# Modulation units behind one counter, placed over more stages, and their quadrants added in five parts, in a two-block transformer kernel in fp32 on one core

## The chip, the cores and the metric

One core of one Trainium2 chip. The metric is the device time of one launch in microseconds (us), the median of repeated runs. A matrix product runs on TensorE (PE); VectorE (DVE), ScalarE (ACT) and GpSimd (POOL) work beside it, and SyncE (SP) issues most of the transfers.

## The reference, cut to what matters

Two models follow one another, each two layers deep, on 256 tokens of width 1024, all in fp32. The first has multi-head latent attention, sliding-window attention, and squared-ReLU MLPs. The second has a gated convolution and recurrence layer, then a stick-breaking attention layer, both with SwiGLU feed-forwards. Each layer of the second is modulated by a vector that depends on `c` alone:

```python
def ada_modulation(c, ada_w, ada_b):                 # c: (1, 1024), ada_w: (1024, 6144)
    m = jax.nn.silu(c) @ ada_w + ada_b
    return jnp.split(m, N_MOD, axis=-1)              # six vectors of 1024

def even_layer(x, c, ada_w, ada_b, mix_norm, w_in, ...):
    sh_m, sc_m, g_m, sh_f, sc_f, g_f = ada_modulation(c, ada_w, ada_b)
    h = modulate(rms_norm(x, mix_norm), sh_m, sc_m)
    ...
    x = x + g_m[:, None, :] * y
    hf = modulate(rms_norm(x, ffn_norm), sh_f, sc_f)
    return x + g_f[:, None, :] * swiglu(hf, ffn_w_gate, ffn_w_up, ffn_w_down)
```

The odd layer does the same with its own `ada_w`. Each of the two `ada_w` matrices is 24 MB; they are multiplied by one vector.

## The kernel before, in words

**The weights' ring.** Activations lie transposed: features on the partitions, 256 tokens in a row. Every large weight streams through a ring of two slots. For a slot SP loads `raw`; ScalarE rounds it to `w_hi` in two halves (`split`, L745, which waits for the load and for TensorE's earlier use of the slot); VectorE subtracts, `w_lo = raw - w_hi` (`split`, L1260, also two halves); TensorE multiplies three times for each chunk, hi by hi, hi by lo and lo by hi (L2172, L2173, L2174). A full slot is a block of 96 matmuls of 128x256, half of them for one pair of feature rows, half for the other (`two_bank_slot`, L2234). It waits for both halves of `w_lo`, and for the earlier contents of its PSUM banks to have been taken (`wait_acc`).

**The order of work.** All engines run programs written out by hand, in the same order of stages: w_o0, up0, down0, swa, w_o1, up1, down1 of the first model (`mlp` holds up and down, `swa` is the sliding-window layer); then lru_in, gate_up0, ffn_down0, qkv, the stick-breaking attention, sb_out, gate_up1, ffn_down1 of the second. Within an engine nothing overtakes: an instruction that waits holds up all behind it. `add_to_residual` and `add_gated` (L1464) on VectorE add the products to `xT`; the norm's first pieces follow from that (L1441 is the last step of the residual sum, L2053 the sum in ffn_down).

**Modulation.** The product with `ada_w` is not done on TensorE but on VectorE, in 96 units. A unit is one transfer of 512 KB (issued by POOL, `ada_load`, L571, into one of two buffers; it waits until unit m - 2 has been used) and two operations on VectorE (`ada_unit`, L1758 or L1761) that multiply by a column of silu(c) and add. Four units make one of 24 groups. A finished group (`ada_group_done`) is transposed into PSUM bank 7 (L1779) and reduced (L1782) into `ada_part`; the semaphore `ada_summed` counts groups. PSUM bank 7 is shared with the scores of the sliding-window heads, so TensorE waits for `ada_summed` ahead of `heads(16, 32)`. Of a finished layer `ada_combine` (four small matmuls, L2230) adds the quadrants into the norm bank, and `modulation` on VectorE adds the bias (L1789) and makes the gains of the two norms (L1791).

A table, `ADA_GROUP`, gives each stage its fixed units, in pairs (`ada_units`): a pair in each of w_o0's two turns, in each j of up and down, and so on. In up, gate_up0 and the turns of ffn_down VectorE's program is a hardware loop (`Fori`) around `hidden` or `turns`. `ada_combine(0)` runs inside up1, behind its fourth slot; `ada_combine(1)` in ffn_down0 behind the first `down`; `modulation(0)` stands in down1 at j = 1, `modulation(1)` in ffn_down0.

Where the pairs stand on VectorE's queue: in w_o0 and w_o1 the second pair stands behind all sums and ahead of `mlp`, whose first act is `split(Slot("up", 1))`. In down0 and down1 the pair of j = 7 stands ahead of the sum of the second turn's first two banks. In swa one pair stands behind split 2, ahead of the distances and the second queries; the other stands behind split 3, ahead of `swa_kT` (L1884), the keys of heads 16 and on. ScalarE swaps their halves (L1037) before TensorE forms the scores of heads 16 and 17 (L2422, `score_head`), for which it waits for `k_ready`.

## Time and profile before

| what | value |
| --- | --- |
| median of 3 runs | 1190.78 us (1190.17, 1190.78, 1193.43) |
| the profiled execution's own time | 1182.13 us |
| its span in the trace | 1180.5 us |
| TensorE busy | 1156.9 us, 98% of the span |
| VectorE busy | 881.7 us, 75% |
| ScalarE busy | 634.3 us, 54% |
| GpSimd busy | 95.6 us, 8% |
| moved by the DMA engines | 248.97 MB, mean 211 GB/s |
| granted TensorE clock | full in all of the 40 slices |

Busy time is the union of the records of an engine's instructions; matmuls are pipelined, so their records overlap, and 98% is not 98% of the peak. A row of a timeline gives the start, the length, the engine and line, the tiles and shapes, and in square brackets how long the engine was idle before and what ended that. The trace has one profiled execution, whose time is not the median's.

### The profile page before, as it was taken

How to read it: one execution, taken by the hardware profiler on the slowest of the kernel's cores; microseconds unless marked ns; L12 is line 12 of the kernel's file. 1: busy time of each engine (PE TensorE's matmuls, PEld its weight loads, DVE VectorE, ACT ScalarE, POOL GpSimd, SP SyncE). 2: the span in 40 equal slices, each digit the busy share in tenths (PEclk: the TensorE clock that was granted, in tenths of full speed). 3: DMA queues.
4: the chain of work that ended last, by engine and by line, in shares of the span. 5: the costliest groups of instructions: out<-in, count | busy, mean ns of one | idle time of the engine just before them, and what ended most of it. 6: DMA issues, size and time to landing. Idle time of an engine off the chain costs nothing.

```text
span 1180.5 us, 23101 instructions
## 1 busy us (share of the span) xinstructions
PE 1156.9 (98%) x9525; PEld 1119.7 (95%) x9525; DVE 881.7 (75%) x1174; ACT 634.3 (54%) x853; POOL 95.6 (8%) x147
## 2 busy tenths in 40 slices
PE   8999999999989999999999999999999999999998
PEld 8999999999988999999999999999988879999998
DVE  5876898878876798888998888887576557855543
ACT  7558566633347567634468463443455574634332
POOL 0000011111124011111200001010000000000000
PEclk9999999999999999999999999999999999999999
DMA  9352588887772488788844657877645504565462
GB/s 329 138 179 73 190 292 272 312 308 235 263 267 72 157 275 305 273 302 294 306 167 143 198 159 253 281 265 240 207 165 172 199 1 143 186 206 180 146 196 85
DMA packets 150060, 248.97 MB, mean 211 GB/s; under 512 B 5553, under 2 KB 80922, under 8 KB 149978
## 3 DMA queue, kind: packets, MB, share of 16 engines
q1 hardware_dynamic: 135858, 197.17, 49.6%
q0 software_dynamic: 13952, 50.60, 11.8%
q8 instruction: 60, 0.98, 0.4%
q14 instruction: 22, 0.18, 0.0%
q10 hardware_dynamic: 168, 0.04, 0.0%
HBM read 246.74 MB, written 1.05 MB: 210 GB/s over the span
## 4 chain that ended last, share of the span: by engine, by line
PE 67%; DVE 17%; ACT 4%; issue 3%; DMA 3%; POOL 0%; DVEq 0%; POOLq 0%; ACTq 0%
PE ps L2172 19%; PE ps L2173 19%; PE ps L2174 19%; DVE w_lo L1260 7%; DVE scratch L1761 4%; DMA ada_raw<-in_l_ada_w 3%; ACT w_hi L745 2%; PE ps L2454 2%; PE ps L2320 1%; PE ps L2764 1%; PE ps L2436 1%; DVE ps L1779 1%; ACT h_both L812 1%; PE ps L2738 1%; PE ps L2423 1%
## 5 line engine op out<-in xcount | busy, mean ns | idle before, releaser
L1260 DVE TENSOR_TENSOR w_lo<-raw,w_hi 128x2048 fp32r<-128x2048 f32 (+4 forms) x196 | 412.7, 2144 | 88.4 <-ACT w_hi L745 87.9
L745 ACT ACTIVATE w_hi<-raw 128x2048 fp32r<-128x2048 f32 (+4 forms) x196 | 342.2, 1791 | 156.4 <-PE ps L2174 151.9
L2172 PE MATMUL ps<-h_both,w_hi 128*128 128x256 f32 (+1 forms) x1296 | 360.6, 278 | 7.9 <-DVE w_lo L1260 4.4
L2173 PE MATMUL ps<-h_both,w_hi 128*128 128x256 f32 (+1 forms) x1296 | 358.8, 277 | 0.0
L2174 PE MATMUL ps<-h_both,w_lo 128*128 128x256 f32 (+1 forms) x1296 | 358.7, 277 | 0.0
L2172 PEld LDWEIGHTS ps<-h_both,w_hi 128*128 128x128 f32 (+1 forms) x1296 | 242.7, 187 | 9.9 <-issue 5.0
L2173 PEld LDWEIGHTS ps<-h_both,w_hi 128*128 128x128 f32 (+1 forms) x1296 | 243.4, 188 | 0.1
L2174 PEld LDWEIGHTS ps<-h_both,w_lo 128*128 128x128 f32 (+1 forms) x1296 | 242.7, 187 | 0.0
L2172 PE MATMUL ps<-a_both,w_hi 128*128 128x256 f32 x864 | 238.8, 276 | 0.6 <-DVE xT L2053 0.6
L2173 PE MATMUL ps<-a_both,w_hi 128*128 128x256 f32 x864 | 238.5, 276 | 0.0
L2174 PE MATMUL ps<-a_both,w_lo 128*128 128x256 f32 x864 | 238.5, 276 | 0.0
L2172 PEld LDWEIGHTS ps<-a_both,w_hi 128*128 128x128 f32 x864 | 162.2, 188 | 0.8 <-DVE xT L2053 0.8
L2173 PEld LDWEIGHTS ps<-a_both,w_hi 128*128 128x128 f32 x864 | 162.2, 188 | 0.0
L2174 PEld LDWEIGHTS ps<-a_both,w_lo 128*128 128x128 f32 x864 | 162.2, 188 | 0.0
L1761 DVE SCALAR_TENSOR_TENSOR scratch<-ada_raw,silu_c,scratch 128x512 f32<-128x512 f32 x168 | 126.2, 751 | 13.6 <-DMA ada_raw<-in_l_ada_w 6.1
L571 POOL DMA_DIRECT2D ada_raw<-in_l_ada_w x96 | 69.5, 724 | 623.6 <-DVE scratch L1761 623.3
L1153 ACT ACTIVATE a_both<-a_full 128x512 fp32r<-128x512 f32 x18 | 11.4, 633 | 107.5 <-DVE a_full L2038 107.5
L1007 ACT ACTIVATE a_full<-ps 128x512 f32<-128x512 f32 x32 | 19.0, 595 | 51.2 <-PE ps L2174 51.1
L2172 PE MATMUL ps<-h_wide,w_hi 128*128 128x258 f32 x160 | 45.8, 286 | 0.2 <-DVE xT L1441 0.2
L2173 PE MATMUL ps<-h_wide,w_hi 128*128 128x258 f32 x160 | 45.4, 284 | 0.0
L2174 PE MATMUL ps<-h_wide,w_lo 128*128 128x258 f32 x160 | 45.3, 283 | 0.0
L2172 PE MATMUL ps<-w_hi,h_both 128*128 128x512 f32 (+1 forms) x112 | 42.8, 382 | 0.7 <-issue 0.7
(423 smaller groups left out, 1806.6 us busy)
## 6 DMA issues: line engine op xcount, KB each, us to landing
ada_raw<-in_l_ada_w POOLq DMA_DIRECT2D x96, 512.0 KB, 6.9
raw<-in_mlp_w_up SPq DMA_DIRECT2D x32, 1024.0 KB, 6.4
raw<-in_mlp_w_down SPq DMA_DIRECT2D x32, 1024.0 KB, 6.9
raw<-in_l_ffn_w_gate SPq DMA_DIRECT2D x22, 1024.0 KB, 5.4
raw<-in_l_ffn_w_up SPq DMA_DIRECT2D x22, 1024.0 KB, 8.6
raw<-in_l_ffn_w_down SPq DMA_DIRECT2D x16, 768.0 KB, 6.0
raw<-in_l_w_qkv SPq DMA_DIRECT2D x12, 1024.0 KB, 6.9
raw<-in_l_w_in SPq DMA_DIRECT2D x10, 1024.0 KB, 6.3
```

The lines of the kernel that those rows point to most:

```text
L571: pool.dma_start(ada_raw[:, slot, :, :], ada[l][:, 2 * quarter:2 * quarter + 2, group])\
L745: nc.scalar.activation(w_hi[:, s.slot, cut], raw[:, s.slot, cut], ACT.Copy).then_inc(split_hi, 1)
L812: ins = nc.scalar.activation(h_hi[:, ch, :], xT[:, ch, :], ACT.Copy, scale=col_a[:, gain_at + ch:gain_at + ch + 1])
L1007: nc.scalar.activation(full, acc(b if j else FIRST_UP_BANKS[b]).rearrange("p (c t) -> p c t", c=2), ACT.Relu)\
L1260: nc.vector.tensor_tensor(w_lo[:, s.slot, cut], raw[:, s.slot, cut], w_hi[:, s.slot, cut].bitcast(F32), ALU.subtract).then_inc(split_lo, 1)
L1761: ins = nc.vector.scalar_tensor_tensor(ada_sum, w, c, ada_sum, ALU.mult, ALU.add)
L1779: nc.vector.transpose(ps[:, ADA_BANK, :], ada_sum).then_inc(ada_turned, 1)
L2172: nc.tensor.matmul(to, sh, mh, start=first, stop=False, skip_group_check=True)
L2173: nc.tensor.matmul(to, sh, ml, start=False, stop=False, skip_group_check=True)
L2174: return nc.tensor.matmul(to, sl, mh, start=False, stop=last, skip_group_check=True)
L2320: ins = nc.tensor.transpose(ps[0:ncols, bank, ch * T + t * P:ch * T + (t + 1) * P], src(ch, t), ident[:, :])
L2454: ins = nc.tensor.matmul(ps[:, 6 + g % 2, qt * T + j * HD:qt * T + (j + 1) * HD], p[:, n * P:(n + 1) * P], v, start=j == 0 and n == 0, sto ...
```

## The change

One counter, `ada_begun`, hands out the units in order: `ada_units(n)` runs the next n, and closes a group with every fourth. The stages take other numbers of units than before (the calls in the diff), and `UP_UNITS` gives those of the up stages. VectorE's hardware loops are written out. `MOD_PARTS` cuts the 24 groups into five parts (first group, end, which gain is made): each has its own `ada_combine(k)` on TensorE and `modulation(k)` on VectorE, and `mod_kept` keeps a combine from writing over a part that VectorE has not taken. POOL's loads keep their order; they are cut at other points around its other work.

```diff
-ADA_GROUP = {"w_o0": 0, "up0": 1, "down0": 5, "swa": 9, "w_o1": 10, "up1": 11, "down1": 15, "gate_up0": 19}
+MOD_PARTS = ((0, 8, 0), (8, 12, 1), (12, 18, 0), (18, 22, 1), (22, 24, None))
+UP_UNITS = ((1, 1, 2, 2, 2, 2, 2, 2), (1, 1, 1, 2, 2, 2, 1, 2))
...
-            ada_loads(0, 10)
+            ada_loads(0, 8)
...
-            ada_loads(10, 11)
+            ada_loads(8, 11)
             ada_pair(11, 1)
             ada_pair(12, 0)
-            ada_loads(12, 19)
+            ada_loads(12, 15)
...
-            ada_loads(19, 23)
-            ada_pair(23, 1)
+            ada_loads(15, 21)
...
             nc.gpsimd.tensor_copy(denied[:, :], suffix[:, :]).then_inc(pool_step, 1)
+            ada_loads(21, 23)
+            ada_pair(23, 1)
...
-            def ada_units(phase, j, i=None):
-                slot_no = 2 * ADA_GROUP[phase] + j
...
-                for u in range(2):
-                    ada_unit(grow(4, 2 * slot_no + u), u, 2 * (j % 2) + u, grow(32, 16 * (slot_no + 1)))
-                if j % 2:
-                    layer = ADA_GROUP[phase] > ADA_GROUP["w_o1"] if i is not None else slot_no // 2 >= ADA_GROUPS
-                    ada_group_done(grow(1, slot_no // 2 + 1), ADA_SLOTS if layer else 0)
...
+            ada_begun = [0]
+            def ada_units(n):
+                for m in range(ada_begun[0], ada_begun[0] + n):
+                    ada_unit(m)
+                    if m % 4 == 3:
+                        ada_group_done(m // 4)
+                ada_begun[0] += n
+            def ada_group_done(g):
+                dve.wait_ge(ada_step, 8 * (g + 1))
                 nc.vector.transpose(ps[:, ADA_BANK, :], ada_sum).then_inc(ada_turned, 1)
...
+                dve.wait_ge(ada_turned, g + 1)
+                nc.vector.tensor_reduce(ada_part[:, g % ADA_GROUPS, :], ps[:, ADA_BANK, :].rearrange("p (b k) -> p b k", k=32),
+                                        AX.X, ALU.add).then_inc(ada_summed, 1)
...
-            def modulation(l):
...
-                dve.wait_ge(ada_combined, l + 1)
-                link(nc.vector.tensor_tensor(mod[:, l, :], ps[:, NORM_BANK, T:T + 48], col_b[:, c:c + 48], ALU.add))
...
+            def modulation(k):
+                first, last, which = MOD_PARTS[k]
+                l, at, n = first // ADA_GROUPS, 4 * (first % ADA_GROUPS), 4 * (last - first)
+                c = COL_B[f"ada_b{l}"] + at
+                dve.wait_ge(ada_combined, k + 1)
+                nc.vector.tensor_tensor(mod[:, l, at:at + n], ps[:, NORM_BANK, T:T + n], col_b[:, c:c + n], ALU.add).then_inc(mod_kept, 1)
+                dve.wait_ge(mod_kept, k + 1)
+                if which is not None:
+                    key = ("mix", "ffn")[which] + str(l)
+                    link(nc.vector.scalar_tensor_tensor(modg[:, l, which, :], mod[:, l, 8 + 24 * which:16 + 24 * which], 1.0,
+                                                        col_a[:, COL_A[key]:COL_A[key] + KD], ALU.add, ALU.mult))
...
             split(Slot("w_o0", 1))
-            ada_units("w_o0", 0)
+            ada_units(2)
             add_to_residual("w_o0", 0, following="mlp0")
             split(Slot("w_o0", 2))
             add_to_residual("w_o0", 1, following="mlp0")
-            ada_units("w_o0", 1)
             def mlp(l):
...
                 split(Slot(f"up{l}", 1))
                 delayed_sum(f"mlp{l}", 3)
...
-                def hidden(i):
...
-                                ada_units(f"up{l}", j, i)
-                        split(Slot(f"up{l}", j + 2, i, 2))
-                hidden(None)
+                def hidden(j):
...
+                        if b == 0:
+                            ada_units(UP_UNITS[l][j])
+                    split(Slot(f"up{l}", j + 2))
+                for j in range(2):
+                    hidden(j)
...
-                hidden(1)
-                if l:
-                    dve.wait_ge(ada_combined, 1)
-                with dve.Fori(2, 4) as i:
-                    hidden(i)
-                for j in range(8):
+                for j in range(2, 8):
+                    hidden(j)
+                for j in range(7):
                     if l and j == 1:
...
-                    ada_units(f"down{l}", j)
+                    ada_units(2)
                     following = ("attn1", "final")[l]
                     if j == 3:
                         add_to_residual(f"down{l}", 0, following, pairs=(0,))
-                    if j < 7:
-                        split(Slot(f"down{l}", j + 2))
+                    split(Slot(f"down{l}", j + 2))
                     if j == 3:
                         add_to_residual(f"down{l}", 0, following, pairs=(1,))
...
             swa_queries(0)
             split(Slot("swa", 2))
-            ada_units("swa", 0)
+            ada_units(2)
...
             swa_queries(1)
             split(Slot("swa", 3))
-            ada_units("swa", 1)
             wait_part(Slot("swa", 2), 0)
             nc.vector.tensor_tensor(swa_kT[:, :, :], two(SWA_BANKS[2][0]), row_pair, ALU.mult).then_inc(acc_out[0], 1)
...
             split(Slot("swa", 5))
-            ada_units("w_o1", 0)
+            ada_units(2)
             add_to_residual("w_o1", 0, following="mlp1")
             split(Slot("swa", 6))
             add_to_residual("w_o1", 1, following="mlp1")
-            ada_units("w_o1", 1)
             mlp(1)
...
             split(Slot("lru_in", 3))
+            modulation(1)
             for b in range(2):
...
-                    if l == 0:
-                        ada_units(f"gate_up{l}", j - 2, i)
+                    if j < 10 or l == 0:
+                        ada_units(2 - l)
                     dve.wait_ge(parts_done, s.before + 2)
...
-                with dve.Fori(1, 4) as i:
-                    for j in range(2):
-                        hidden(j, i)
-                for j in (8, 9, 10):
+                for j in range(2, 11):
                     hidden(j)
...
-                if l == 0:
-                    ada_units("gate_up0", 9)
-                    split(Slot("ffn_down0", 2))
-                    add(0)
-                    split(Slot("ffn_down0", 3))
-                    modulation(1)
-                    turns(1)
-                else:
-                    turns(0)
+                if l:
+                    modulation(4)
+                for i in range(3):
+                    if l == 0:
+                        ada_units(2)
+                    split(Slot(f"ffn_down{l}", 2 * i + 2))
+                    add(i)
+                    split(Slot(f"ffn_down{l}", 2 * i + 3))
+                    if l == 0 and i == 0:
+                        modulation(2)
                 if l == 0:
...
                 if j < 5:
                     split(Slot("qkv", j + 2))
+                if 1 <= j < 5:
+                    ada_units(1)
             def capped(pair):
...
             split(Slot("sb_out", 1))
+            modulation(3)
             add_gated("sb_out", 0, 1, "ffn1")
...
-            def ada_combine(l):
-                pe.wait_ge(quadrants_ready, 1)
-                pe.wait_ge(ada_summed, ADA_GROUPS * (l + 1))
-                first = 1 - l
...
+            def ada_combine(k):
+                first, last, _ = MOD_PARTS[k]
+                pe.wait_ge(ada_summed, last)
+                if k:
+                    pe.wait_ge(mod_kept, k)
+                at, n = first % ADA_GROUPS, 4 * (last - first)
+                part = ada_part[:, at:at + last - first, :].rearrange("p g (c j) -> p (g c) j", j=4)
...
+                with pe.Fori(1, 4) as i:
+                    two_bank_slot(f"up{l}", 0, i, 2)
+                    two_bank_slot(f"up{l}", 1, i, 2)
                 if l:
-                    for j in (2, 3):
-                        two_bank_slot("up1", j)
+                    pe.wait_ge(quadrants_ready, 1)
                     pe.wait_ge(norm_var, NORM_AT["mlp1"] + 1)
                     ada_combine(0)
-                with pe.Fori(1 + l, 4) as i:
-                    two_bank_slot(f"up{l}", 0, i, 2)
-                    two_bank_slot(f"up{l}", 1, i, 2)
...
-            pe.wait_ge(ada_summed, 10)
+            pe.wait_ge(ada_summed, 8)
...
             lru_slot(1, second_free)
+            pe.wait_ge(norm_var, NORM_AT["final"] + 1)
+            ada_combine(1)
             lru_slot(2, taken((0, 1), (1, 0)))
...
+                if l:
+                    ada_combine(4)
                 if l == 0:
                     down(0)
-                    ada_combine(1)
+                    ada_combine(2)
                     with pe.Fori(1, 4) as i:
                         down(i)
                 else:
...
                 pe.wait_ge(w_exped, 2 * pair + 2)
+                if pair == 2:
+                    pe.wait_ge(ada_summed, 22)
...
             as_chunks_arrive("sb_out", 3)
+            ada_combine(3)
             two_bank_slot("sb_out", 1)
```

## Rows read from the trace of the kernel before

**Rows 1.** The page, part 1: busy us, share of the span, instructions of each engine.

```profile
PE 1156.9 (98%) x9525; PEld 1119.7 (95%) x9525; DVE 881.7 (75%) x1174; ACT 634.3 (54%) x853; POOL 95.6 (8%) x147
```

**Rows 2.** Timeline, VectorE in `gate_up1`: start, us, operation, idle before and its releaser.

```profile
1039.29 0.69 DVE L2038 TENSOR_TENSOR a_full<-a_full,ps 128x512 f32 x1 [3.19 <-PE ps L2174]
...
1050.18 0.69 DVE L2038 TENSOR_TENSOR a_full<-a_full,ps 128x512 f32 x1 [3.20 <-PE ps L2174]
```

**Rows 3.** Timeline, TensorE: first matmuls behind five pauses.

```profile
151.61 0.39 PE L2172 MATMUL ps<-h_both,w_hi 128*128 128x256 f32 x1 [1.96 <-DVE w_lo L1260]
...
317.23 0.36 PE L2172 MATMUL ps<-h_both,w_hi 128*128 128x256 f32 x1 [1.66 <-DVE xT L1441]
...
350.25 0.34 PE L2422 MATMUL ps<-swa_kT,swa_qT 64*128 64x128 f32 x1 [3.34 <-DVE qx L1890]
...
421.49 0.38 PE L2172 MATMUL ps<-h_both,w_hi 128*128 128x256 f32 x1 [1.94 <-DVE w_lo L1260]
...
587.56 0.39 PE L2172 MATMUL ps<-h_wide,w_hi 128*128 128x258 f32 x1 [0.18 <-DVE xT L1441]
```

**Rows 4.** Timeline, ScalarE: split ahead of `up0` 1, and swapped keys in `swa`.

```profile
142.02 3.71 ACT L745 ACTIVATE w_hi<-raw 128x2048 fp32r<-128x2048 f32 x2
...
349.52 0.63 ACT L1037 ACTIVATE swa_kT_swapped<-swa_kT 64x512 f32<-64x512 f32 x1
```

**Rows 5.** Timeline, VectorE behind the sums of w_o0.

```profile
142.50 3.18 DVE L1761 SCALAR_TENSOR_TENSOR scratch<-ada_raw,silu_c,scratch 128x512 f32<-128x512 f32 x4
...
147.08 4.48 DVE L1260 TENSOR_TENSOR w_lo<-raw,w_hi 128x2048 fp32r<-128x2048 f32 x2
```

**Rows 6.** Timeline, VectorE at the end of down0, and in `swa`.

```profile
311.09 3.18 DVE L1761 SCALAR_TENSOR_TENSOR scratch<-ada_raw,silu_c,scratch 128x512 f32<-128x512 f32 x4 [1.36 <-DMA ada_raw<-in_l_ada_w]
...
343.49 3.22 DVE L1761 SCALAR_TENSOR_TENSOR scratch<-ada_raw,silu_c,scratch 128x512 f32<-128x512 f32 x4 [2.42 <-DMA ada_raw<-in_l_ada_w]
...
348.11 0.68 DVE L1884 TENSOR_TENSOR swa_kT<-ps,r_row 128x512 f32<-128x512 f32 x1
```

**Rows 7.** Timeline, VectorE in `gate_up0`: splits of two slots in turn.

```profile
774.28 4.49 DVE L1260 TENSOR_TENSOR w_lo<-raw,w_hi 128x2048 fp32r<-128x2048 f32 x2 [1.00 <-ACT w_hi L745]
...
784.70 4.49 DVE L1260 TENSOR_TENSOR w_lo<-raw,w_hi 128x2048 fp32r<-128x2048 f32 x2 [1.11 <-ACT w_hi L745]
```

**Rows 8.** Timeline, TensorE: around a combine; stick-breaking's first sums; `sb_out` block 0's end.

```profile
454.60 0.28 PE L2174 MATMUL ps<-h_both,w_lo 128*128 128x256 f32 x1
...
455.09 0.39 PE L2172 MATMUL ps<-h_both,w_hi 128*128 128x256 f32 x1
...
940.76 0.48 PE L2764 MATMUL ps<-sb_sp,suffix 128*128 128x384 f32 x1
...
980.77 0.28 PE L2174 MATMUL ps<-h_both,w_lo 128*128 128x256 f32 x1
```

**Rows 9.** Timeline, VectorE: `modulation` in ffn_down0, the stick-breaking's begin, `sb_out`.

```profile
820.46 0.20 DVE L1789 TENSOR_TENSOR mod<-ps,col_b 128x48 f32<-128x48 f32 x1
820.69 0.24 DVE L1791 SCALAR_TENSOR_TENSOR modg<-mod,col_a 128x8 f32<-128x8 f32 x2
...
934.05 1.02 DVE L2138 TENSOR_SCALAR sb_l<-ps 128x384 f32<-128x384 f32 x2 [0.63 <-PE ps L2742]
...
936.28 1.01 DVE L2147 TENSOR_TENSOR sb_sp<-ps,sb_l 128x384 f32<-128x384 f32 x2
...
979.73 0.87 DVE L1464 SCALAR_TENSOR_TENSOR xT<-ps,mod,xT 128x256 f32<-128x256 f32 x2 [2.76 <-PE ps L2174]
```

**Rows 10.** Windows: stretch, length, busy of PE, PEld, DVE, ACT, POOL, clock, DMA share, GB/s.

```profile
346.00:351.00 5.00, 1.66 (x17) 1.27 (x15) 3.48 (x6) 2.08 (x3) 3.57 (x7) 1.00 1.03 390
816.00:862.00 46.00, 45.45 (x406) 45.22 (x402) 25.05 (x26) 20.33 (x17) 0.00 (x0) 1.00 0.64 217
```

**Rows 11.** Timeline, ScalarE in ffn_down0.

```profile
810.59 2.66 ACT L745 ACTIVATE w_hi<-raw 128x1408 fp32r<-128x1408 f32 x2 [4.46 <-DMA raw<-in_l_ffn_w_down]
...
832.06 2.65 ACT L745 ACTIVATE w_hi<-raw 128x1408 fp32r<-128x1408 f32 x2 [4.83 <-PE ps L2174]
```

More of the change, by code:

```diff
@@ L1750, in _, with ada_unit @@
             ada_sum = scratch[:, 2:4, :].rearrange("p c t -> p (c t)")
[L1752 to L1754 removed]
+            def ada_unit(m):
+                slot, quarter = m % 2, m % 4
+                dve.wait_ge(ada_loaded[slot], 16 * (m // 2 + 1))
                 for q in range(2):
@@ L1810, in mlp @@
                 delayed_sum(f"mlp{l}", 3)
-                def hidden(i):
-                    grow = (lambda per, first: first) if i is None else (lambda per, first: i * per + first)
-                    for j in range(2):
-                        for b in range(2):
-                            at_pair = bass.ds(i * 8 + (4 * j + 2 * b), 2) if i is not None else slice(4 * j + 2 * b, 4 * j + 2 * b + 2)
-                            dve.wait_ge(hid_hi, grow(4, HIDDEN_BEFORE[str(l)] + 2 * j + b + 1))
-                            nc.vector.tensor_tensor(a_lo[:, at_pair, :], a_full[:, at_pair, :],
-                                                    a_hi[:, at_pair, :].bitcast(F32), ALU.subtract).then_inc(hid_lo, 1)
-                            if b == 0:
-                                ada_units(f"up{l}", j, i)
-                        split(Slot(f"up{l}", j + 2, i, 2))
-                hidden(None)
+                def hidden(j):
+                    for b in range(2):
+                        at_pair = slice(4 * j + 2 * b, 4 * j + 2 * b + 2)
+                        dve.wait_ge(hid_hi, HIDDEN_BEFORE[str(l)] + 2 * j + b + 1)
+                        nc.vector.tensor_tensor(a_lo[:, at_pair, :], a_full[:, at_pair, :],
+                                                a_hi[:, at_pair, :].bitcast(F32), ALU.subtract).then_inc(hid_lo, 1)
+                        if b == 0:
[3 more added lines that the diff above has]
+                    hidden(j)
                 delayed_var(f"mlp{l}")
@@ L2061, in ffn @@
                 split(Slot(f"gate_up{l}", 3))
-                with dve.Fori(1, 4) as i:
-                    for j in range(2):
-                        hidden(j, i)
-                for j in (8, 9, 10):
+                for j in range(2, 11):
                     hidden(j)
-                def turns(first):
-                    with dve.Fori(first, 3) as i:
-                        split(Slot(f"ffn_down{l}", 2, i, 2))
-                        add(i)
-                        split(Slot(f"ffn_down{l}", 3, i, 2))
-                if l == 0:
-                    ada_units("gate_up0", 9)
-                    split(Slot("ffn_down0", 2))
-                    add(0)
-                    split(Slot("ffn_down0", 3))
-                    modulation(1)
-                    turns(1)
-                else:
-                    turns(0)
+                if l:
[8 more added lines that the diff above has]
+                        modulation(2)
                 if l == 0:
```

46 lines of the change are left out of this document (12 added, 34 removed).

## The prediction

> **What bounds the kernel now.** I read the page's first part first. TensorE is busy 98% of the span, VectorE 75% [rows 1]. Matmuls overlap in the records, so the busy share doesn't say how dense TensorE is; the starts of its matmuls do. In `gate_up1` VectorE waits for each block of 96 matmuls, from 1039.29 to 1050.18 [rows 2]: 10.89 us, 0.113 us for each. Elsewhere the starts keep that step but for a few marked pauses. So TensorE sets the time, and a change is worth what it takes from, or adds to, the pauses between its matmuls; VectorE's load matters only where a pause names it.
>
> Next I read TensorE's timeline at the borders of stages. A pause costs its idle time plus 0.17 us (the record before it runs 0.28 us, of which 0.11 is its step). Five pauses stand in front of work that VectorE delivers late [rows 3]:
> - 151.61, block 1 of `up0`, waits for a split: 1.96 + 0.17 = 2.1 us. 421.49 is the same place of the next layer: 2.1 us.
> - 317.23, first matmul of `swa`, waits for the residual sum: 1.8 us. 587.56 is its twin before `lru_in`: 0.35 us.
> - 350.25, the scores of heads 16 and 17: 3.5 us. The row names the queries (L1890); but the swapped keys, which the scores need too, end at 349.52 + 0.63 = 350.15 [rows 4], 0.1 us before.
>
> Together 9.9 us.
>
> Then I read what VectorE did in front of each. At 142.50 it runs two units (four operations, 3.18 us) and closes a group, and only at 147.08 begins the split [rows 5], though ScalarE began its half of that split at 142.02 [rows 4]. At 311.09 two units come after 1.36 us of waiting for their transfer, and the residual sum stands behind them; at 343.49 another pair has waited 2.42 us for its transfer, and `swa_kT` (348.11) stands behind it [rows 6]. At all five places modulation units, whose result is needed much later, run ahead of something that TensorE awaits.
>
> **The change, part by part.** The units stay 96, the groups 24. A pair costs VectorE 3.2 us, closing a group 147.08 - 142.50 - 3.18 = 1.4 us more [rows 5]. Units per stage, before and after: w_o0 4, 2; up0 16, 14; down0 16, 14; swa 4, 2; w_o1 4, 2; up1 16, 12; down1 16, 14; gate_up0 18, 18; ffn_down0 2, 6; qkv 0, 4; gate_up1 0, 8.
>
> *w_o0 and w_o1:* the second pair goes, so the split of `up` 1 can follow ScalarE, whose two halves take 3.71 us together from 142.02, to 145.73 [rows 4]. A half of the split takes 2.24 (4.48 for two [rows 5]): the lower part is there by 145.73 + 2.24 = 148.0. TensorE was ready at 151.61 - 2.1 = 149.5. Both pauses go, with 1.5 us to spare: -4.2 us. Late next would be ScalarE's halves.
>
> *down0 and down1:* the pair of j = 7 goes, so the sum of the first two banks follows its own matmuls, during the second half of the block: -1.8 and -0.35 us. Late next is the split of `swa` 1; it stands behind the same sums and comes sooner with them.
>
> *swa:* one pair instead of two; it now has its group's close (1.4 us), but nothing stands between split 3 and `swa_kT`. Split 3 ends at 343.49 - 2.42 = 341.1; with the close 342.5. From `swa_kT` to the swapped keys took 350.15 - 348.11 = 2.0 us [rows 4, 6], so they are there at 344.6. TensorE asks at 350.25 - 3.5 = 346.7: -3.5 us, 2.1 to spare. TensorE's wait for `ada_summed` asks for 8 groups instead of 10, and 8 are closed by then. POOL is freed of loads sooner (through pair 8 instead of 10) and can build the head biases earlier; two bias buffers set that pace, so I count nothing.
>
> *Loops written out, units in `up`, `down` and `gate_up0`:* the same work in the same order. In `gate_up0` VectorE is as slow as TensorE: 774.28 to 784.70 is 10.4 us for a block [rows 7], 11.8 for one with a close, mean 11.1 against 10.9. It keeps its 18 units, so that stays: 0.
>
> *Combines, five for two:* one costs 455.09 - 454.60 - 0.11 = 0.38 us of TensorE [rows 8]. The moved ones cost nothing new. Added are one in `lru_in`, one before `ffn_down1`, one in `sb_out`. The first two have their inputs long before, and VectorE's half of them (under 0.7 us, 0.20 + 2 x 0.24 [rows 9]) falls into idle stretches: +0.4 and +0.4. The wait on `norm_var` of "final" ahead of `lru_in` 2 is for a value written before that stage's first eviction: 0.
>
> *Added wait, `sb_out`:* this one is not hidden. `modulation(3)` stands on VectorE's queue ahead of the sum of the first bank, and its combine stands on TensorE's queue behind all of block 0. Before, that sum starts at 979.73, while TensorE still fills the second bank; block 0's last matmul starts at 980.77 and block 1 follows in step, at 980.88 [rows 8, 9]. After: that last matmul ends at 980.77 + 0.28, the combine 0.38 later, at 981.4; about 0.1 on, VectorE's two small operations (0.20 + 0.24) and the sum's pair (0.87) run till 982.8, and with 0.1 to hand over TensorE goes on at 982.9 to 983.0 instead of 980.88: +2.1 us, the combine included. The bounds: 0.4 (combine alone, if block 1 could begin in other banks) and 3.5 (the longest pause of its kind, 350.25). The order of the queues says 2.1, nearest to its own rows. The wait ahead of pair 2 of the stick-breaking asks for 22 groups, closed in `qkv`.
>
> *Moved into `ffn_down0`, `qkv` and `gate_up1`:* 18 units where 2 were. In `gate_up1` VectorE idles 3.2 us ahead of each product [rows 2]; one unit takes 1.6, with a close 3.0: hidden, cover 0.2. In `ffn_down0` a pair stands ahead of a split whose buffer TensorE frees. In `qkv` the last unit and its close (3.0) stand ahead of the stick-breaking, whose first operation starts at 934.05 after 0.63 us of idling: 2.4 later. Its first pair of sums then ends not at 936.28 + 1.01 = 937.3 but at 939.7, and TensorE takes it at 940.76 [rows 8, 9]: cover 1.1; without it +2.4 at most. Their transfers go through POOL's queue, 0.5 MB each, in stages where the engines of the DMA are 0.64 busy (`ffn_down0` [rows 10]); SP's weight loads keep their order but share the engines. POOL's last three pairs stand behind its triangles, which are built long before.
>
> Sum: -4.2 - 1.8 - 0.35 - 3.5 + 0.4 + 0.4 + 2.1 = **-7.0 us**. The durations are from the profiled execution, 1182.13 us (span 1180.5, 1.6 around it). The median shown is 1190.78, 0.7% above it; I carry the difference over unchanged: 1190.78 - 7.0 = 1183.8.
>
> *The clock.* Through the pause of 3.5 us the granted clock stays 1.00, the 2.4 GHz level [rows 10], and the new pause is shorter, so I charge nothing for it. The Trainium skill, "TensorE: Matmul & The Clock Gate", Part 1, says that an idle TensorE is throttled to 1.2 GHz. By that sentence the sum would be that of the last rival; the row does not show it.
>
> **Rivals.**
> 1. *The next wait takes the place.* ScalarE's halves or a transfer end about as late as the units did. For it: the cover worked out above is 1.5 to 2.1 us, and units wait for their transfers at two of the five places [rows 6]. Against: [rows 4] puts ScalarE early. If half of each pause comes back: -4.9 + 2.9 = -2.0, 1188.8 us.
> 2. *The `sb_out` wait is covered.* Only the combine is paid: -7.0 - 1.7 = -8.7, 1182.1 us. Against: the first bank is awaited.
> 3. *Slower: late weights in `ffn_down0`.* ScalarE once waited 4.46 us for a weight transfer there (810.59 [rows 11]), just where units were still being loaded. The change has six units there. If three blocks come 4.46 late each, 13.4: -7.0 + 13.4 = +6.4, 1197.2 us. It decides once a load takes over 11.5 us: from the split that frees the buffer, done by 820.46 [rows 9], to its use at 832.06 [rows 11].
> 4. *Slower: the clock falls at the new pause* and block 1 of `sb_out` takes twice its 10.9 us: -7.0 + 10.9 = +3.9, 1194.7 us. Against: [rows 10].
>
> **How the numbers follow.** A measurement of this kernel tells 0.3%, 3.6 us, from no change. Chances: forecast 0.66, rival 1 0.18, rival 2 0.10, rival 3 0.04, rival 4 0.02. Faster is forecast and rival 2, 0.76; same is rival 1, 0.18; slower is rivals 3 and 4, 0.06. The range takes in rivals 1 and 2, at the far ends widened by 0.7 and 2.1 for the runs' own spread (1190.17 to 1193.43) and the bounds of `sb_out`: 1180.0 to 1189.5.
>
> **What would show it.** No pause over 0.3 us at the first matmuls of block 1 of `up0` and `up1` and of `swa` and `lru_in`; the scores of heads 16 and 17 right behind the features; a new pause of about 2 us behind the combine in `sb_out`, ended by L1464's sum; none new in `qkv`, `gate_up1`, `ffn_down0`. I am wrong if the first five remain, if a wait for `w_hi` or a transfer stands there, or if the stages that take the units grow by more than 1 us each.

## The result and the profile after

The change does not make the kernel faster: 1194.8 us (14 executions, 1194.37 to 1196.32) against 1191.05 us (14 executions, 1185.89 to 1195.36), a ratio of 1.0031, 95% interval 1.0017 to 1.0045. Forecast were 1183.8 us and a range up to 1189.5. The 0.3% by which it is slower is small beside what the kernel before does by itself: beside the experiments below its median lies between 1189.90 and 1195.70. What has to be explained is the gain of 7 us that did not come.

Every pause that the change was to remove is gone all the same. The page of the changed kernel, part 1, and TensorE's timeline at the places of [rows 3] and in `sb_out`:

```profile
PE 1179.1 (99%) x9549; PEld 1143.3 (96%) x9549; DVE 882.9 (74%) x1177; ACT 635.1 (53%) x853; POOL 98.4 (8%) x147
```

```profile
151.24 0.28 PE L2159 MATMUL ps<-h_both,w_lo 128*128 128x256 f32 x1
151.36 0.28 PE L2157 MATMUL ps<-h_both,w_hi 128*128 128x256 f32 x1
...
319.37 0.28 PE L2159 MATMUL ps<-a_both,w_lo 128*128 128x256 f32 x1
319.48 0.28 PE L2157 MATMUL ps<-h_both,w_hi 128*128 128x256 f32 x1
...
349.94 0.28 PE L2159 MATMUL ps<-h_both,w_lo 128*128 128x256 f32 x1
350.15 0.37 PE L2409 MATMUL ps<-swa_kT,swa_qT 64*128 64x128 f32 x1
...
419.88 0.28 PE L2159 MATMUL ps<-h_both,w_lo 128*128 128x256 f32 x1
420.00 0.28 PE L2157 MATMUL ps<-h_both,w_hi 128*128 128x256 f32 x1
...
588.42 0.28 PE L2159 MATMUL ps<-a_both,w_lo 128*128 128x256 f32 x1
588.53 0.28 PE L2157 MATMUL ps<-h_wide,w_hi 128*128 128x258 f32 x1
...
985.38 0.26 PE L2217 MATMUL ps<-ada_part,line_h 128*32 128x16 f32 x8
987.14 0.36 PE L2157 MATMUL ps<-h_both,w_hi 128*128 128x256 f32 x1 [1.50 <-DVE xT L1466]
```

No bracket stands at the first five places, and one behind the combine, 1.50 us, where the prediction put it. But one kind of step, the time from a matmul's start to the next start, has grown: 151.24 to 151.36, behind a matmul that reads `h_both`, is 0.12 us, where [rows 2] give 0.113; 319.37 to 319.48, behind one that reads `a_both`, is still 0.11. So I counted the matmuls of the same 20 us in `up0`, `down0` and `gate_up1`. Windows of the kernel before, then of the changed one (columns as in [rows 10]):

```profile
200.00:220.00 20.00, 20.00 (x179) 20.00 (x178) 17.61 (x18) 12.72 (x16) 2.90 (x4) 1.00 0.79 280
260.00:280.00 20.00, 20.00 (x179) 20.00 (x178) 14.34 (x15) 8.78 (x7) 2.17 (x3) 1.00 0.80 293
1060.00:1080.00 20.00, 20.00 (x178) 20.00 (x178) 11.75 (x8) 9.70 (x8) 0.00 (x0) 1.00 0.64 205
```

```profile
200.00:220.00 20.00, 20.00 (x169) 20.00 (x168) 17.34 (x17) 12.80 (x13) 1.45 (x2) 1.00 0.73 256
260.00:280.00 20.00, 20.00 (x179) 20.00 (x178) 14.90 (x18) 6.00 (x6) 2.90 (x4) 1.00 0.80 281
1060.00:1080.00 20.00, 20.00 (x169) 20.00 (x169) 14.66 (x13) 8.63 (x7) 1.43 (x2) 1.00 0.64 207
```

TensorE is 100% busy in all six, at full clock. In `up0` and `gate_up1`, whose products read `h_both`, the changed kernel gets 169 matmuls into 20 us where 179 and 178 went before; in `down0`, which reads `a_both`, the count is the same. Busy share and clock say nothing of this; only the count or the starts do. Of the 3888 steps behind a matmul of `features` (the function that multiplies a block of weights by 256 tokens) that reads `h_both`, 614 took 0.116 to 0.125 us before and 3831 after, nearly all of these 0.120; longer ones, which are waits, are left out of all such counts here.

### The profile page after: what moved, and what is told of

Same layout as the page of the kernel before. It is cut to its first block, busy times and chain, and to the rows that moved or that the text cites. A ratio compares the mean times of both kernels' runs of the same rounds, so it can differ in the third digit from the quotient of the medians.

```text
span 1193.0 us, 22907 instructions
## 1 busy us (share of the span) xinstructions
PE 1179.1 (99%) x9549; PEld 1143.3 (96%) x9549; DVE 882.9 (74%) x1177; ACT 635.1 (53%) x853; POOL 98.4 (8%) x147
## 4 chain that ended last, share of the span: by engine, by line
PE 92%; DVE 1%; issue 0%; POOL 0%; ACT 0%; DVEq 0%
PE ps L2157 28%; PE ps L2159 27%; PE ps L2158 27%; PE ps L2441 2%; PE ps L2307 1%; PE ps L2754 1%; PE ps L2423 1%; PE ps L2728 1%; PE ps L2410 1%; PE ps L2770 1%; PE ps L2242 0%; PE ps L2409 0%; DVE w_lo L1262 0%; PE ps L2755 0%; PE ps L2732 0%
## 5 line engine op out<-in xcount | busy, mean ns | idle before, releaser
L2157 PE MATMUL ps<-h_both,w_hi 128*128 128x256 f32 (+1 forms) x1296 | 367.9, 284 | 2.6 <-DVE xT L1466 1.5
L2158 PE MATMUL ps<-h_both,w_hi 128*128 128x256 f32 (+1 forms) x1296 | 366.6, 283 | 0.0
L2159 PE MATMUL ps<-h_both,w_lo 128*128 128x256 f32 (+1 forms) x1296 | 366.6, 283 | 0.0
L2157 PEld LDWEIGHTS ps<-h_both,w_hi 128*128 128x128 f32 (+1 forms) x1296 | 247.9, 191 | 3.6 <-issue 3.3
L2158 PEld LDWEIGHTS ps<-h_both,w_hi 128*128 128x128 f32 (+1 forms) x1296 | 248.0, 191 | 0.1
L2159 PEld LDWEIGHTS ps<-h_both,w_lo 128*128 128x128 f32 (+1 forms) x1296 | 248.0, 191 | 0.0
```

What stands on the lines that cost most here:

```text
L2157: nc.tensor.matmul(to, sh, mh, start=first, stop=False, skip_group_check=True)
L2158: nc.tensor.matmul(to, sh, ml, start=False, stop=False, skip_group_check=True)
L2159: return nc.tensor.matmul(to, sl, mh, start=False, stop=last, skip_group_check=True)
```

## The experiments

The sum of the prediction has no term for this, so something in the diff had been left out of it. It is these lines, which neither the diff above nor the prediction has:

```diff
-ADA_SLOTS = ADA_GROUPS + 1
-        line_h = sb("line_h", [P, 48])
+        line_h = sb("line_h", [P, 64])
-        ada_part = sb("ada_part", [P, ADA_SLOTS, 16])
+        ada_part = sb("ada_part", [P, ADA_GROUPS, 16])
```

`line_h` lies directly ahead of `h_wide` and `h_both` in SBUF, and `ada_part` behind them and ahead of the arena, which holds `a_both`. 16 words more in one place and 16 less in the other move `h_both` up by 64 bytes and leave the arena where it was. Worked out from the sizes in the source, `h_both` begins 64 bytes above a multiple of 128 before and on a multiple of 128 after; the arena begins 64 above one in both, the weights' tiles `w_hi` and `w_lo` on one.

**The place alone, both ways.** `old_line` is the changed kernel with the 16 words moved from `line_h` to a pad ahead of `ada_part`:

```diff
-        line_h = sb("line_h", [P, 64])
+        line_h = sb("line_h", [P, 48])
+        sb("line_m", [P, 16])
         ada_part = sb("ada_part", [P, ADA_GROUPS, 16])
```

> The changed kernel with its padding moved by 16 words, so that the activations h_both begin 64 bytes lower, where the kernel before has them; schedule, units and combines stay as changed. Theory A (the place of h_both sets TensorE's step): in the trace of the changed kernel 3831 of the 3888 steps behind a matmul that reads h_both take about 0.120 us, in that of the kernel before 614, and the quick ones 0.113. With the old place the 3217 steps become quick again, 3217 x 0.0067 = 21.5 us: 1194.8 - 21.5 = 1173.3 us, in any case 1168 to 1181, steps 0.113 in the up stages, gate_up0 and gate_up1. Theory B (a pause in front of a block lets TensorE fall into the quick step, and the change took the pauses away): no pause comes back here, so the steps stay 0.120 and the time 1194.8, within 2 us. Theory C (the written-out order of the units is what slows TensorE): 1194.8 as well.

Measured: 1181.61 us (1173.86 to 1181.93), ratio to the kernel before 0.9896 (0.9858 to 0.9934); the profiled execution took 1173.86. Only 69 steps at `h_both` are slow in it. Theory A holds, B and C fall: no pause and no loop came back. The profiled execution is where theory A put it (1173.3); the median lies 0.6 us above its range, for a reason that shows further down.

`before_moved` is the kernel before with `final_gain` and `silu_c` defined ahead of `h_wide`.

```diff
         line_h = sb("line_h", [P, 48])
...
+        final_gain = sb("final_gain", [P, KD])
+        silu_c = sb("silu_c", [P, KD])
         h_wide = sb("h_wide", [P, 2, KD, T + 2], F32R)
...
-        final_gain = sb("final_gain", [P, KD])
...
-        silu_c = sb("silu_c", [P, KD])
```

> The kernel before, with two small tensors (64 bytes together) moved from behind h_both to ahead of it, so that h_both begins where the changed kernel has it; nothing else. Theory A: 3274 quick steps become slow, 0.0067 us each, 21.9 us, on the kernel before's own time: 1203 to 1214 us, steps 0.120 at h_both while the five pauses of the kernel before are all still there. Theories B and C: 1191, within 4 us, steps 0.113.

Measured: 1206.06 us, 12.0 over the kernel before in the same runs, ratio 1.0106 (1.0058 to 1.0155), 3810 slow steps at `h_both`. Windows of `old_line`, then of `before_moved`, in `up0` and `down0`:

```profile
200.00:220.00 20.00, 20.00 (x179) 20.00 (x179) 16.71 (x19) 12.72 (x16) 2.89 (x4) 1.00 0.79 282
260.00:280.00 20.00, 20.00 (x179) 20.00 (x178) 16.25 (x16) 8.12 (x7) 1.44 (x2) 1.00 0.70 254
```

```profile
200.00:220.00 20.00, 20.00 (x169) 20.00 (x168) 15.64 (x15) 14.66 (x16) 2.17 (x3) 1.00 0.78 289
260.00:280.00 20.00, 20.00 (x179) 20.00 (x178) 15.61 (x16) 4.18 (x4) 2.89 (x4) 1.00 0.77 281
```

**Whose place?** `arena_moved` is the changed kernel with `rsum` and `sinkexp` (64 bytes) ahead of the arena, `weights_moved` the changed kernel with the 16 words between `raw` and `w_hi`:

```diff
+        rsum = sb("rsum", [P, NT, 4])
+        sinkexp = sb("sinkexp", [P, NT, 4])
         arena = sb("arena", [P, 16384])
...
-        rsum = sb("rsum", [P, NT, 4])
-        sinkexp = sb("sinkexp", [P, NT, 4])
```

```diff
         raw = sb("raw", [P, 2, SLOT])
+        sb("line_w", [P, 16])
...
-        line_h = sb("line_h", [P, 64])
+        line_h = sb("line_h", [P, 48])
```

> The changed kernel with the arena, which holds a_both and o_hi/o_lo, 64 bytes higher; h_both stays. If a start of 64 above a multiple of 128 bytes is the quick place for any operand that TensorE reads by rows of 256 words, the 2568 steps at a_both and 378 at o_hi and o_lo go from 0.113 to 0.120: +19.7 us, 1214.5 us (1210 to 1219). If h_both alone is special (or B or C hold): 1194.8 within 2 us, a_both at 0.113.

> The changed kernel with 64 bytes put between raw and w_hi instead of ahead of h_both: w_hi, w_lo, ada_raw and xT begin 64 bytes higher, h_both and the arena stay where the changed kernel has them. If what counts is the place of the activations against that of the weights (unlike by 64 bytes: quick), h_both becomes quick, 0.113, and a_both slow, 0.120: -21 + 19.7, about 1193 us, told by the steps and not by the time. If the place of the activations alone counts: h_both stays 0.120, a_both 0.113, 1194.8 within 2 us. If the weights' place has a price of its own, both change: over 1200 or under 1180.

`arena_moved` took 1214.48 us, ratio 1.0179 (1.0131 to 1.0228): no matmul that reads `a_both` or `o_hi`/`o_lo` has a quick step any more. `weights_moved` took 1191.27 us, 0.999 (0.9964 to 1.0015): `h_both`, not moved, has 3222 quick steps again, and of the 2592 at `a_both`, not moved either, 2100 are slow. So it is the place of the activations against that of the weights that counts: 64 bytes apart within 128 is quick, the same place within 128 is slow. The last case is not quite like the others, though. The steps at `a_both` there are no even 0.120 but spread from 0.114 to 0.122, 0.1187 on average. By the sizes `a_both` begins 128 bytes off the weights within 256 there, while in the three kernels with an even 0.120 (the changed one, `before_moved`, `arena_moved`) the two begin at the same place within 256. No run tried this difference by itself. Windows of `arena_moved`, then of `weights_moved`:

```profile
200.00:220.00 20.00, 20.00 (x169) 20.00 (x169) 15.89 (x15) 14.30 (x16) 2.17 (x3) 1.00 0.75 281
260.00:280.00 20.00, 20.00 (x169) 20.00 (x169) 15.38 (x15) 4.75 (x3) 2.89 (x4) 1.00 0.72 255
```

```profile
200.00:220.00 20.00, 20.00 (x179) 20.00 (x178) 17.84 (x18) 12.73 (x16) 2.89 (x4) 1.00 0.78 280
260.00:280.00 20.00, 20.00 (x171) 20.00 (x170) 13.50 (x15) 8.72 (x7) 2.42 (x4) 1.00 0.85 311
```

**How far?** `place_96` is `old_line` with 8 of the 16 words back in `line_h` (`h_both` 96 above a multiple of 128); `place_192` is the changed kernel with `final_gain` and `silu_c` ahead of `h_wide` (192 above a multiple of 256):

```diff
-        line_h = sb("line_h", [P, 48])
+        line_h = sb("line_h", [P, 56])
...
-        sb("line_m", [P, 16])
+        sb("line_m", [P, 8])
```

```diff
         line_h = sb("line_h", [P, 64])
...
+        final_gain = sb("final_gain", [P, KD])
+        silu_c = sb("silu_c", [P, KD])
         h_wide = sb("h_wide", [P, 2, KD, T + 2], F32R)
...
-        final_gain = sb("final_gain", [P, KD])
...
-        silu_c = sb("silu_c", [P, KD])
```

> old_line with h_both 32 bytes higher, half way between the place of the kernel before (64 above a multiple of 128) and that of the changed kernel (a multiple of 128). If only whole steps of 64 count: like one of the two, h_both at 0.113 (1174 to 1182 us) or at 0.120 (1195). If the cost grows with the overlap of what TensorE reads for weights and activations: between, about 0.116 to 0.118 at h_both, 1184 to 1192.

> The changed kernel with h_both 64 bytes higher than the change put it, by two small tensors moved ahead of it: 192 above a multiple of 256, where the kernel before has it at 64. If only the place within 128 bytes counts against that of the weights: as old_line, h_both at 0.113 or 0.118, 1173 to 1182 us. If the place of the kernel before is quick for its place within 256: h_both at 0.120, about 1195.

`place_96`: 1194.63 us, 1.0036 (1.0009 to 1.0063). The time is that of the changed kernel, but the steps at `h_both` are not: they spread from 0.115 to 0.123, 0.1183 on average against its 0.1199. What this saves (3888 x 0.0016 = 6 us) is not seen in the time, in the profiled execution mostly because 907 steps at `a_both` are slow, against 17 in the changed kernel. So neither expectation is met as a whole. `place_192`: 1189.49 us, 0.996 (0.9934 to 0.9986). Its steps at `h_both` are 0.113 (946) or about 0.118 (2925), never 0.120 but for 4. That is neither expectation: a third value, 0.118, which the place of the kernel before shows as well. Whether the two places are worth the same is open: the eight executions of `place_192` (1187.00 to 1192.86) lie above all but one of the fourteen of `old_line`.

In the traces with the quick place 0.118 holds, as a rule, from one irregularity of TensorE's (a wait, the begin of a stage) to the next, for up to 1397 steps (`place_192`); the exception is a short stretch near 24 us that ends in an unbroken stream. It falls differently in each execution: 69 slow steps at `h_both` in `old_line`'s profile, 2009 in that of the same kernel profiled again (`old_line_again`). Windows of the first, then of the second, in `up1`:

```profile
440.00:460.00 20.00, 20.00 (x179) 20.00 (x179) 16.64 (x19) 12.72 (x16) 2.89 (x4) 1.00 0.72 253
```

```profile
440.00:460.00 20.00, 20.00 (x172) 20.00 (x172) 16.12 (x15) 12.88 (x14) 2.17 (x3) 1.00 0.68 230
```

With those at the other tiles the second profile has 3605 more of them, 0.0044 us each, which covers the 13.1 us between the two executions (1173.86 and 1186.96). This is most of why `old_line` runs from 1173.86 to 1188.93 while the changed kernel, slow wherever it reads `h_both`, stays within 2 us.

**The kernel before once more, and a pause put back.** `before_again` has no edit. The seventeen executions of the kernel before beside the first four runs showed mean clocks below 1.000, unlike [rows 10]. `pause` puts work in front of `swa_kT`:

```diff
+        idle_work = at("idle_work", 12864, [P, 1536])
...
             split(Slot("swa", 3))
             wait_part(Slot("swa", 2), 0)
+            link(nc.vector.memset(idle_work[:, :], 0.0))
+            for _ in range(3):
+                link(nc.vector.tensor_scalar(idle_work[:, :], idle_work[:, :], 1.0, None, ALU.mult))
```

> The kernel before, unchanged, profiled a second time. Seventeen executions of it beside the last runs showed a mean granted clock of 0.993 to 0.999 and 1187 to 1199 us, while its first profile showed 1.000 and 1182 us. Theory P (its pauses of about 2 us and more let TensorE's clock fall to the lower level in most executions, which the first profile did not show): this profile has a mean clock of 0.994 to 0.998, with the lost clock right behind the pauses before block 1 of up0 and up1, before swa and before the scores of heads 16 and 17, and a span 3 to 10 us over 1180.5. Rival: the lower clock lies anywhere, or behind the start, with no bond to these places.

> The kernel old_line with four operations of about 1.5 us added on VectorE ahead of swa_kT, on memory that nothing reads: the scores of heads 16 and 17 come late again. Of about 5.8 us some 2.1 are cover, so TensorE idles about 3.7 us at this one place. If a pause costs its idle time alone: old_line plus 3.7 us in the profile, mean clock 1.000. If the clock falls behind it (theory P): plus 3.7 and about 1.7 us more, clock 0.55 to 0.6 for some 4 us right behind the pause, mean 0.998 to 0.999, in most of its executions.

`before_again`: 1190.19 us, the profiled execution 1196.87 (span 1195.2, mean clock 0.996). TensorE's timeline behind its two longest pauses, and the windows there (the clock is the third column from the right):

```profile
320.15 0.55 PE L2172 MATMUL ps<-h_both,w_hi 128*128 128x256 f32 x1 [4.01 <-DVE xT L1441]
...
355.30 0.34 PE L2422 MATMUL ps<-swa_kT,swa_qT 64*128 64x128 f32 x1 [3.19 <-DVE qx L1890]
```

```profile
312.00:316.00 4.00, 4.00 (x37) 3.95 (x35) 1.85 (x3) 0.00 (x0) 0.00 (x0) 1.00 1.07 352
316.00:320.00 4.00, 0.14 (x2) 0.00 (x0) 3.86 (x6) 0.00 (x0) 1.45 (x2) 0.83 0.99 258
320.00:324.00 4.00, 3.85 (x18) 3.88 (x19) 2.92 (x7) 3.96 (x5) 0.00 (x0) 0.50 0.42 125
324.00:328.00 4.00, 4.00 (x31) 4.00 (x31) 2.67 (x4) 1.58 (x4) 0.00 (x0) 0.81 0.01 4
348.00:352.00 4.00, 4.00 (x37) 3.91 (x35) 3.21 (x5) 0.00 (x0) 0.72 (x1) 1.00 1.04 376
352.00:356.00 4.00, 0.81 (x9) 0.56 (x8) 2.56 (x5) 2.03 (x3) 3.10 (x6) 1.00 1.04 391
356.00:360.00 4.00, 4.00 (x22) 3.84 (x20) 1.53 (x8) 4.00 (x7) 3.20 (x3) 0.57 0.11 42
360.00:364.00 4.00, 4.00 (x37) 3.87 (x37) 0.00 (x0) 1.03 (x5) 0.00 (x0) 1.00 0.02 4
```

At 320 the granted clock is 0.50, the 1.2 GHz level, and 18 matmuls start where 37 do from 312 to 316. What is missing from 1.00 in these windows is 4 x (0.17 + 0.50 + 0.19 + 0.43) = 5.2 us, but a part of that lies in the idle time itself, where it costs nothing: by their starts, against `old_line`, the matmuls behind the two pauses lose 2.6 and 1.5 us, 4.1 together. Behind the idle times of 1.96 us in `up0` and `up1` nothing is missing here, so theory P holds for two of its four places. `before_moved`'s profile has a clock of 0.57 from 324 to 328 behind an idle time of 2.28 us before `swa`; the first profile of the kernel before has 1.00 behind 3.34. So the length of a pause alone does not tell whether the clock falls. 78 of the 85 executions of the kernel before that were timed beside the experiments have a mean clock under 0.999; the 14 of the changed kernel all have 0.999 or more. The first profile of the kernel before was one of the few without the loss.

The pause before `swa` is also longer here, 4.01 us idle against 1.66 [rows 3], because the pair of units in front of it waits longer for its transfer, 3.70 us against 1.36 [rows 6]:

```profile
314.01 3.18 DVE L1761 SCALAR_TENSOR_TENSOR scratch<-ada_raw,silu_c,scratch 128x512 f32<-128x512 f32 x4 [3.70 <-DMA ada_raw<-in_l_ada_w]
```

Of the 14.7 us by which this span exceeds the first one's, about 4 are thus the clock and 2 the pauses; the largest part, about 7, are 1557 more steps of 0.118.

`pause`: TensorE idles 2.80 us at 345.99, and the stage `swa` lasts 4.4 us longer than in `old_line` (70.08 against 65.69): 2.9 for the pause and 1.5 for the clock, which the windows behind it show. The median, 1181.85, doesn't tell this from the play of 0.113 and 0.118.

```profile
344.00:348.00 4.00, 2.01 (x12) 1.51 (x13) 2.22 (x8) 3.34 (x4) 0.08 (x1) 0.82 0.57 211
348.00:352.00 4.00, 4.00 (x28) 4.00 (x27) 0.51 (x4) 3.38 (x9) 2.26 (x2) 0.75 0.00 0
```

**Towards a better version.** Three kernels take `old_line` and hide the wait in `sb_out` by putting its combine into block 0 (first diff), and lighten `gate_up0` in three ways (second, third and fourth).

```diff
-            as_chunks_arrive("sb_out", 3)
-            ada_combine(3)
+            as_chunks_arrive("sb_out", 3, between=3)
...
+                    if p == 2 and between is not None:
+                        ada_combine(between)
```

```diff
-UP_UNITS = ((1, 1, 2, 2, 2, 2, 2, 2), (1, 1, 1, 2, 2, 2, 1, 2))
+UP_UNITS = ((1, 1, 2, 2, 2, 2, 2, 2), (1, 1, 2, 2, 2, 2, 2, 2))
...
-                        ada_units(2 - l)
+                        ada_units(1 if l or j in (4, 6) else 2)
```

```diff
-                        ada_units(2 - l)
+                        ada_units(1 if l or j in (4, 7, 9) else 2)
...
-                        ada_units(2)
+                        ada_units(3)
                     split(Slot(f"ffn_down{l}", 2 * i + 2))
```

```diff
-                        ada_units(2 - l)
+                        ada_units(1 if l or j in (4, 6, 8, 10) else 2)
...
-                if 1 <= j < 5:
-                    ada_units(1)
+                if j < 5:
+                    ada_units((2, 2, 2, 1, 1)[j])
```

> old_line with two more edits: the combine of part 3 goes between the third and the last quarter of block 0 of sb_out, and one unit each of gate_up0's fifth and seventh slots goes back into up1. The pause of 1.69 us behind the combine goes (old_line's stage is 1.94 us longer than before's; 0.4 of it, the combine itself, stays): -1.5 us. gate_up0's three pauses of 0.84 to 1.01 us, where VectorE with two units and a group's close is slower than TensorE, shrink to one or none: -1.5 to -2.4. Together -3 to -4: 1177.6 to 1178.6 against old_line's median of 1181.6, or 1169 to 1171 in an execution like its profiled one. If the step of TensorE alone sets what is left: no difference from old_line.

`best` (two units of `gate_up0` in `up1`) took 1179.17 us, 0.9909 (0.9876 to 0.9942). It leaves one group open over `lru_in`, whose norm uses the same scratch, so it gets this group's sums wrong; the amount of work is the same.

> old_line with the combine of part 3 between the third and last quarter of block 0 of sb_out, and three units of gate_up0 moved into ffn_down0, one to each turn, so that no group stays open across a stage that uses the same scratch. The stage sb_out is to last about 0.4 us longer than in the kernel before instead of 1.94, and gate_up0 to lose its three pauses of 0.84 to 1.01 us: -3 to -4 us for the same steps, 1177.6 to 1178.6 as a median if TensorE's steps fall into 0.113 and 0.118 as they did in old_line's runs (1173.9 to 1181.9).

`best2` (three units in `ffn_down0`) took 1194.32 us, 0.9984 (0.9954 to 1.0014), about 16 us more than expected. The third unit of a turn has no transfer under way, since there are two buffers; VectorE waits for it, and the split and the sum (L2044) behind it, for which TensorE waits, are late. VectorE in `best2`:

```profile
800.70 0.75 DVE L1765 SCALAR_TENSOR_TENSOR scratch<-ada_raw,silu_c,scratch 128x512 f32<-128x512 f32 x1
806.45 1.54 DVE L1765 SCALAR_TENSOR_TENSOR scratch<-ada_raw,silu_c,scratch 128x512 f32<-128x512 f32 x2 [4.99 <-DMA ada_raw<-in_l_ada_w]
807.90 3.15 DVE L1263 TENSOR_TENSOR w_lo<-raw,w_hi 128x1408 fp32r<-128x1408 f32 x2
```

TensorE idles 4.86 and 4.82 us in two of three turns, ended by that sum, the clock falls to 0.50 behind both, and `ffn_down0` is 15 us longer than in `old_line`.

> old_line with the combine of part 3 between the third and last quarter of block 0 of sb_out, and four units moved from gate_up0 (18 to 14) to qkv (4 to 8; two in each of its first three slots, one in the next two, so that none is the third at its place and has to wait for its own transfer, as the third unit did in best2 for 5 us). For the same steps: sb_out 1.2 us shorter than in old_line, gate_up0 2 to 2.7 us shorter, qkv unchanged if VectorE's idle time there covers two more units a slot, or up to 3 us longer if it doesn't. Median 3 us under old_line's in the same session, less what chance does to TensorE's steps (0.113 or 0.118, up to 8 us in one execution).

> old_line once more, beside best3: what the schedule of the change alone is worth, with h_both at the place of the kernel before. By the idle times of the five pauses alone: -7 to -8 us against the kernel before, -0.6 to -0.7%. If the clock falls behind two or more of these pauses in most executions of the kernel before and in none of this one: 3 to 7 us more, -0.9 to -1.3%, and mean clocks of 0.999 to 1.000 here beside 0.994 to 0.998 there.

`best3` (four units in `qkv`, at most two at a place) took 1179.91 us, 0.9897 (0.9863 to 0.9931), faster than both kernels; `old_line_again` beside it 1183.59, 0.992 (0.9887 to 0.9953), between its two expectations; its mean clocks are 0.999 to 1.000. In `best3` the sum in `sb_out` waits for its product alone, and the stage lasts 22.62 us, 0.75 longer than before instead of `old_line`'s 1.94:

```profile
972.95 0.17 DVE L1792 TENSOR_TENSOR mod<-ps,col_b 128x16 f32<-128x16 f32 x1 [1.94 <-PE ps L2218]
973.15 0.17 DVE L1796 SCALAR_TENSOR_TENSOR modg<-mod,col_a 128x8 f32<-128x8 f32 x1
974.56 0.88 DVE L1467 SCALAR_TENSOR_TENSOR xT<-ps,mod,xT 128x256 f32<-128x256 f32 x2 [1.24 <-PE ps L2160]
```

`gate_up0` shows no pause in it, but its steps are 0.118 throughout in this profile. Chance in the steps is larger than what is left to gain, so `best3` is not told from `old_line` by their medians.

## Why the prediction was wrong

Three profiled executions, each cut at the first matmul of a stage (the starts come from the timelines; us, and the difference to the kernel before):

```
stage                 before    after   old_line    after   old_line
                          length in us              against before
up0                    89.75    92.56    87.50      +2.81    -2.25
down0                  88.87    87.06    87.04      -1.81    -1.83
swa                    69.42    67.16    65.69      -2.26    -3.73
up1                    90.22    92.89    87.83      +2.67    -2.39
gate_up0              126.09   128.68   125.67      +2.59    -0.42
sb_out                 21.88    25.05    23.82      +3.17    +1.94
gate_up1              123.27   128.69   123.58      +5.43    +0.31
all others            563.89   563.86   563.92      -0.03    +0.03
```

*The pauses.* By `old_line` each term was right: `up0` -2.25 and `up1` -2.39 (forecast -2.1 each), `down0` -1.83 (-1.8), `swa` -3.73, of which -3.41 at the scores (-3.5). `sb_out` is +1.94 (+2.1), the combines in `lru_in` and before `ffn_down1` +0.28 and +0.27 (+0.4 each). By the spans the sum is 1172.3 - 1180.5 = -8.2 against the -7.0 forecast; -0.4 each in `gate_up0` and `ffn_down0` (a pause of 0.7 us less) are the largest of the rest. In `gate_up0` two things meet: the kernel before has 478 steps of 0.118 there, 2.1 us, and `old_line` two more waits for VectorE, 0.9 and 0.6 us, where the prediction had put 0.

*The step that failed* is the list of the parts itself. "Sum" adds pauses and takes the step of 0.113 for granted ("Elsewhere the starts keep that step", which 614 steps did not quite do even before). The matmuls' own step has no term, so a change of it stood at nothing without a reason. Nothing in the prediction asked what else the diff moves: two tiles resized, which I took for bookkeeping of the groups. The runs show the missing term as the difference between the profiles of the changed kernel and of `old_line`, 1193.0 - 1172.3 = 20.7 us, 5.1 in each of `up0`, `up1` and `gate_up1`. In `gate_up0` it is only 3.0, since `old_line` there waits for VectorE three times, and the slower TensorE of the changed kernel does not. One sign of being wrong that the prediction named came true by this: `gate_up1`, which takes units, grew by 5.4 us, through the step and not through the units.

*The clock.* "I carry the difference over unchanged" and "I charge nothing for it" failed as well, the other way. One execution with a clock of 1.00 was taken for the kernel; in most executions the clock falls behind pauses that the change takes away. In `before_again` that is 4.1 us more in its favour, and 2.2 for longer pauses, which the profiles of before and after could not show. The last rival had the mechanism and the wrong place: the new pause of 1.50 us shows no lower clock in the changed kernel, and its price was the removed pauses'. The Trainium skill, "TensorE: Matmul & The Clock Gate", Part 1, says that an idle TensorE is put back to 1.2 GHz: `before_again` agrees, with 0.50 behind an idle time of 4.01 us; the first profile, with 1.00 behind 3.34, shows that not every such pause does it.

*The medians.* The schedule alone gives 1181.6 and 1183.6 us against 1194.0 and 1192.5 beside them, -12.4 and -8.9 us, with intervals of -17.0 to -7.9 and -13.5 to -5.6. So the gain from the schedule is shown; that it is more than the forecast -7.0, as pauses and clock together would have it, is not, since the second interval holds -7.0 and the steps of 0.118 fall by chance in both kernels. The place of `h_both` puts back 11 to 13 us in the medians (1194.8; 12.0 in `before_moved`), less than 20.7, since part of `old_line`'s steps are 0.118 in most executions.

*The rivals.* None was it. That the last one's 1194.7 us is almost the measured 1194.8 is chance: the clock of the changed kernel stayed at 1.00. Rival 1's waits did not come, nor rival 2's cover; rival 3 did not occur with two units a turn (`ffn_down0` -0.7 us) and did in `best2` with three, though at the unit's own transfer and not at the weights'. Moved units cost nothing in `qkv`, and in `gate_up1` at most the +0.3 us of `old_line`.

## What to carry to other kernels

Read every line of a diff that gives a tile another size, and work out which tiles behind it move: here, in the profiles, 64 bytes were worth twice the five pauses together. Where TensorE is 100% busy, count its matmuls in equal windows before and after; the step shows what busy share and clock hide. And look at the mean clock of several executions before one profile is taken for the kernel, as a pause costs more than its idle time in those where the clock falls.

## What the runs showed that I had not expected

A 128x256 product of two fp32r operands steps at 0.113 us where the activations begin 64 bytes off the weights within 128, and at 0.120 where they begin at the same place within 256: 6%, in either tile (`h_both`, `a_both`). Moving the weights instead of the activations switches it too. In between, 32 bytes off the quick place (`place_96`) or at the same place within 128 but not within 256 (`weights_moved`), the steps spread around 0.118 and 0.119. At the quick place there is a second value, 0.118, that as a rule sets in or ends only where TensorE's stream is broken and lasts hundreds of matmuls. What makes the choice between 0.113 and 0.118, and what in the memory makes the difference of 64 bytes, was not tried and stays open.
